# Value pages of the sample attention in two places per chunk step instead of three: a hybrid decoder step on one core

## What is computed

```
def step(S, xs):
    u_c, w_c, attn_c, q_c, k_c, gl = xs
    v_new = u_c - w_c @ S
    o = q_c @ S + attn_c @ v_new
    S = S * jnp.exp(gl)[..., None, None] + jnp.einsum('bhck,bhcv->bhkv', k_c, v_new)
    return S, o
```

```
v_past = v_pool[page_table].reshape(db, past, HA, DVA)
a = p[:, :, 0] - lam * p[:, :, 1]
return jnp.einsum('bhk,bkhe->bqhe', a.astype(v.dtype), v)
```

## Time and profile before

| | |
|---|---|
| median of 3 runs | 2679.56 us (2677.13 to 2680.27) |
| profiled execution | 2676.61 us, span 2674.4 us |
| TensorE busy | 98% of the span, granted clock 0.995 |
| vector, scalar, GpSimd busy | 57%, 43%, 51% |
| DMA | 138 GB/s over the span |
| the chunk loop from its second step | about 597 to 743 us of the span |

### The profile page before, as it was taken

How to read it: one execution, slowest core, us unless ns; L and a number is a source line. 1 busy time by engine, 2 the same in 40 slices (tenths; PEclk the granted TensorE clock), 3 DMA queues, 4 the chain that set the end, 5 groups by cost and what they waited for, 6 DMA issues and landing times.

```text
span 2674.4 us, 46814 instructions
## 1 busy us (share of the span) xinstructions
PE 2623.7 (98%) x17245; PEld 2393.9 (90%) x17245; DVE 1522.6 (57%) x2918; ACT 1149.1 (43%) x1777; POOL 1351.6 (51%) x614
## 2 busy tenths in 40 slices
PE   8999999989999999999999999999999999999998
PEld 5886666667776999999999999999999999999998
DVE  4227868865467333343347885378863788635323
ACT  2227739955523433343333424344343432444333
POOL 0210015621011766667666776676766767665663
PEclk9999999989999999999999999999999999999999
DMA  5220057635693544444444444544444544444553
GB/s 184 69 94 9 17 167 223 205 99 157 174 287 102 160 136 137 138 139 142 141 142 134 134 142 137 147 135 137 138 129 140 145 138 138 134 134 134 157 152 94
DMA packets 457191, 368.99 MB, mean 138 GB/s; under 512 B 15501, under 2 KB 400114, under 8 KB 456732
## 3 DMA queue, kind: packets, MB, share of 16 engines
q1 hardware_dynamic: 444846, 347.05, 44.2%
q0 software_dynamic: 2992, 12.26, 1.5%
q10 hardware_dynamic: 9174, 7.22, 0.9%
HBM read 351.17 MB, written 17.14 MB: 138 GB/s over the span
## 4 chain that ended last, share of the span: by engine, by line
PE 90%; DVE 4%; ACT 2%; DMA 2%; issue 1%; SPq 0%; POOL 0%; DVEq 0%; ACTq 0%
PE bank L3035 21%; PE bank L3037 21%; PE bank L3036 21%; PE bank L1232 6%; PE bank L2527 3%; PE bank L1973 2%; PE bank L922 2%; PE bank L372 1%; PE bank L524 1%; PE bank L523 1%; PE bank L522 1%; PE bank L902 1%; PE bank L873 1%; PE bank L1863 1%; DVE tmp L2903 1%
## 5 line engine op out<-in xcount | busy, mean ns | idle before, releaser
L3494 POOL TENSOR_TENSOR wl<-wring,wh 128x1024 fp32r<-128x1024 f32 x466 | 1137.5, 2456 | 589.0 <-ACT wh L3251 588.7
L3035 PE MATMUL bank<-xh,wh 128*128 128x344 f32 x2688 | 862.7, 321 | 0.3 <-POOL wl L3494 0.3
L3037 PE MATMUL bank<-xh,wl 128*128 128x344 f32 x2688 | 858.8, 320 | 0.0
L3036 PE MATMUL bank<-xl,wh 128*128 128x344 f32 x2688 | 857.3, 319 | 0.0
L3251 ACT ACTIVATE wh<-wring 128x1024 fp32r<-128x1024 f32 x466 | 484.1, 1055 | 768.3 <-PE bank L3037 645.4
L3035 PEld LDWEIGHTS bank<-xh,wh 128*128 128x128 f32 x2688 | 505.9, 188 | 1.8 <-POOL wl L3494 0.6
L3037 PEld LDWEIGHTS bank<-xh,wl 128*128 128x128 f32 x2688 | 505.4, 188 | 0.0
L3036 PEld LDWEIGHTS bank<-xl,wh 128*128 128x128 f32 x2688 | 504.3, 188 | 1.2
L3572 DVE TENSOR_TENSOR bank<-bank,gates_tmp 128x344 f32<-128x344 f32 x132 | 69.2, 524 | 511.4 <-PE bank L3037 420.4
L3616 DVE SCALAR_TENSOR_TENSOR bank<-big,vec,bank 128x344 f32<-128x344 f32 (+1 forms) x696 | 354.7, 573 | 0.5
L3035 PE MATMUL bank<-hh,wh 128*128 128x344 f32 x1040 | 334.3, 321 | 3.2 <-DVE hl L3574 3.2
(11 more groups left out here) (463 smaller groups left out, 3118.1 us busy)
## 6 DMA issues: line engine op xcount, KB each, us to landing
wring<-in_ffn_w_down SPq DMA_DIRECT2D x132, 512.0 KB, 3.6
wring<-in_ffn_w_gate SPq DMA_DIRECT2D x131, 512.0 KB, 3.9
wring<-in_ffn_w_up SPq DMA_DIRECT2D x131, 512.0 KB, 3.8
wring<-in_conv_w_pw SPq DMA_DIRECT2D x72, 512.0 KB, 4.1
big<-in_cache_attn_k SPq DMA_DIRECT2D x128, 256.0 KB, 3.0
big<-in_cache_attn_v SPq DMA_DIRECT2D x128, 256.0 KB, 3.0
wring<-in_w_in SPq DMA_DIRECT2D x20, 512.0 KB, 4.0
park<-res_a SPq DMA_DIRECT2D x1, 4128.0 KB, 12.8
```

The lines of the kernel that those rows point to most:

```text
L3035: pe.matmul(bank_out, h, mh, start=(n == 0), stop=False)
L3036: pe.matmul(bank_out, h, ml, start=False, stop=False)
L3037: mm = pe.matmul(bank_out, l, mh, start=False, stop=(n == len(terms) - 1))
L3494: pool.tensor_tensor(wl[s % 6][:, :], raw_w[s % WQ] if raw is None else raw, wh[s % 6][:, :].bitcast(F32), ALU.subtract).then_inc(w_cut, 1)
```

## The change

From `k` = 2 on, the three groups of a step stand in two places. In steps 3, 4, 5, 7 and 8 the first place takes groups `3(k-1)` and `3(k-1)+1`, which belong to one sample, one behind the other into bank 5, the second adding onto the first; the last place keeps the third. In steps 2 and 6, where the step's first group ends a sample, the first place keeps one group and the last place takes two. The middle place and its use of bank 6 are gone, with the waits for it. The vector engine adds a bank once for two groups: two sums in each step instead of three, 17 in the program instead of 24.

```diff
+        def page_groups(pe, gs, n):
+            for g in gs:
+                page_group(pe, g, n, g == gs[0], g == gs[-1])
+
+        def groups_first(k):
+            return (3 * (k - 1),) if k % 4 == 2 else (3 * (k - 1), 3 * (k - 1) + 1)
+
+        def groups_second(k):
+            return (3 * (k - 1) + 1, 3 * (k - 1) + 2) if k % 4 == 2 else (3 * (k - 1) + 2,)
+
-        def page_group(pe, g, n):
+        def page_group(pe, g, n, begin=True, end=True):
...
-                mm = pe.matmul(bank[32 * q:32 * (q + 1), n, :], w, ring[:, pp % 4, u, :], start=True, stop=True)
+                mm = pe.matmul(bank[32 * q:32 * (q + 1), n, :], w, ring[:, pp % 4, u, :], start=begin, stop=end)
             mm.then_inc(vpage_used, STRIPS)
-        def group_copy(dve, g, n):
+        def group_copy(dve, g, n, of=1):
...
-            dve.wait_ge(vpage_used, 8 + STRIPS * (g + 1))
+            dve.wait_ge(vpage_used, 8 + STRIPS * (g + of))
...
-                page_group(pe, 3 * (k - 1), 5)
+                page_groups(pe, groups_first(k), 5)
...
-                    pe.wait_ge(oc_copied, k - 1)
-                else:
-                    pe.wait_ge(k_scaled, k + 1)
-                page_group(pe, 3 * (k - 1) + 1, 6)
...
-                pe.wait_ge(group_in, 3 * k - 2)
+                pe.wait_ge(group_in, groups_first(k)[-1] + 1)
                 values_new(k - 1)
                 left(k, 2)
-                page_group(pe, 3 * (k - 1) + 2, 2 * ((k - 1) % 2) + 1)
-                pe.wait_ge(group_in, 3 * k - 1)
+                page_groups(pe, groups_second(k), 2 * ((k - 1) % 2) + 1)
                 outputs(k - 1)
...
-                group_copy(dve, 3 * (k - 1), 5)
+                group_copy(dve, groups_first(k)[0], 5, len(groups_first(k)))
...
-                group_copy(dve, 3 * (k - 1) + 1, 6)
...
-                group_copy(dve, 3 * (k - 1) + 2, 2 * ((k - 1) % 2) + 1)
+                group_copy(dve, groups_second(k)[0], 2 * ((k - 1) % 2) + 1, len(groups_second(k)))
```

More of the change, by code:

```diff
@@ L1875, in group_copy @@
                     dve.wait_ge(bias_io, 64)
-                dve.tensor_copy(d, src).then_inc(group_in, 1)
+                dve.tensor_copy(d, src).then_inc(group_in, of)
             else:
                 dve.wait_ge(group_in, g)
-                dve.tensor_tensor(d, d, src, ALU.add).then_inc(group_in, 1)
+                dve.tensor_tensor(d, d, src, ALU.add).then_inc(group_in, of)
         def page_column_in(dve, b, n):
```

## The result

| | before | after |
|---|---|---|
| median of 5 runs each | 2677.13 us (2675.00 to 2680.27) | 2694.26 us (2690.05 to 2698.45) |
| profiled execution, its span | 2676.61, 2674.4 us | 2691.74, 2689.9 us |
| mean granted TensorE clock | 0.995 | 0.991 |

The ratio is 1.0059 (1.0047 to 1.0070): slower, by some 16 us. The prediction was +4.3 us on a median of three runs (2679.56; with five it is 2677.13), and its range ended at 2687.4, 7.8 us above that median. So it was wrong; only the sign was right.

A forecast was written before the change was run, and what follows sets the result against it. TensorE, busy 98% of the span, was taken as the bound. Moved groups +4.55, pages +0.35, vector copies -0.42, step 7 +0.44 and `outputs(7)` -0.60 gave +4.3 on 2679.56: 2683.9 us, range 2678.8 to 2687.4.

The forecast's parts named there:

- Nothing is won: Middle place, step 3: without its group `right_turned` starts earlier, but `right(3,1)` still waits until 627.41; no gain.
- Nothing later gives the time back: After the loop: TensorE is dense again, its next wait of 0.19 us moves along, so the loss stays.
- The moved groups: First or last place: a second group costs 0.91 us (0.84 to 1.00), +4.55 over steps 2 to 6.
- rival 1: Added groups at either place find room in TensorE's matmul rows and cost nothing; 2678.5 us, chance 0.12.
- The vector copies: One 0.67 us vector operation fewer per step; removes TensorE's 0.42 us wait in step 3, -0.42.
- The pages: First place, steps 3 and 7: eight pages requested together come late; waits of about 0.35 and 0.37 us.
- Rival 2: Pages come late at the first place's second half in steps 3 and 7; +8.5 us, 2688.1 us, chance 0.20.
- Step 7: Loop step 7: +0.91 for the group, +0.37 page wait, less 0.84 of earlier page waits; +0.44 us.
- Step 8: `outputs(7)` no longer waits for the middle group's sum, -0.60 us; page waits and doubled first place there net 0.
- The sum: Whole kernel: 4.55 + 0.35 - 0.42 + 0.44 - 0.60 = +4.3 us, giving 2683.9 us, +0.16%.

The follow-up runs named there:

- filled run: Changed kernel with four unread 512-column matmuls put into the emptied middle place in each of steps 2 to 7; 2682.43 us, ratio 1.0021.
- the run with the hole filled and narrow groups: Changed kernel with four unread matmuls in the middle place of steps 2 to 7 and each pair's second group cut to 8 columns; 2680.74 us, ratio 1.0016.
- the middle and last place: Page groups in two places per step, the first place given up and the middle kept, against the kernel before; 2699.05 us, ratio 1.0084.

## Why the prediction was wrong

**The step that failed** is "So the group sits in a hole that the two copies make. Take it away and ... Nothing is won." That is true, and incomplete: the emptied place stands in the sum at nothing because no copy ends earlier or later, and what TensorE's idle time there does to its clock was not asked. The hole of 0.73 us was as forecast (0.8), and in step 3 `right(k,1)` comes as long after the last rows of `left(k,1)` as before (627.61 to 629.67, and 625.35 to 627.41 in the earlier trace rows). But in the changed kernel the open hole was followed in steps 2, 4 and 5 by half clock, 1.5 us for each 3.4 us of it. Filling the hole took back some 10 of the 16 us. Step by step the changed kernel is longer than the filled one by 1.48, 0.06, 1.51, 3.08 and 0.00 us in steps 2 to 6, 6.1 together, and by 2.70 in step 7, where the idle stretch told of under **Open** is a part of it. Behind the loop one more stretch at half clock, absent from the kernel before and from the filled run, makes the 16 matmuls of the earlier trace rows last 6.56 us in place of 4.86 (4.87 in the filled run), behind a wait of 0.54 in place of 0.19. Of the 11.2 us between the two spans (2689.9 and 2678.7) these three parts (6.1, 2.7 and 1.7) make 10.5. Only the 6.1 stand right behind the hole in the trace. The last 1.7 need not come from it: with the middle sums dropped and every hole covered the same matmuls took 6.56 us too. Either way "Nothing later gives the time back" had left out that the later work can become slower.

What before had shown on this point I read too narrowly: the earlier trace rows has a hole of 1.03 us in step 8 with no fall of the clock behind it, and I took from it only how long a hole is. One hole without a fall does not tell what one in every step does.

**The moved groups**: 0.87 us each by step lengths (23.12 against 22.25), and 16 records last 1.92 against 1.06. Forecast 0.91 within 0.84 to 1.00: right. The Trainium skill (Perfetto Trace Analysis, "Identifying the Most-Contended Engine") would judge TensorE's room by the share of weight loading, beside the arithmetic done against the peak. In the filled run that was 18.08 of 23.11 us, and each added group still cost its 0.87; here the measurement decides against reading room from that share, and rival 1 falls.

**The vector copies**: the wait of 0.42 in step 3 and that of `outputs(7)` are gone, as forecast; dropping the sums alone gave 0.49 in step 3 and nothing in steps 2 and 4 to 6.

**The pages**: in step 3 the second half of the first place waited 0.39 us (filled run 0.34, forecast 0.35). In step 7 it waited 0.68 in the changed kernel and 1.38 in the filled run (forecast 0.37). Step 7 is a mis-sized term: +1.83 us in the filled run against +0.44, most of it this wait. Rival 2 had the right place and a fraction of its price. Step 8 gained 0.51 there (forecast 0.60).

**The sum**: the loop of the filled run is longer than before by 0.86 + 0.89 + 0.87 + 0.87 + 0.86 + 1.83 - 0.51 = 5.67 us. So the prediction's arithmetic holds to 1.4 us for the kernel that keeps its hole covered, most of that in step 7, and misses the other two thirds of the loss.

**Open.** In step 7 of the changed kernel TensorE stood still for 2.18 us inside `left(7,1)`, and the hole behind it, at the middle place, is not seen. What held TensorE there the profile doesn't name, and no run was made for it; with the hole of step 7 open in the run filled in steps 2 to 4 no such wait came. Why a hole brings the clock down in some steps and not in others is not settled either.

## What to carry to other kernels

Work that stands in a wait can do more than use it: here four page matmuls that cost nothing also kept TensorE's clock up, and taking them out of the wait cost twice, at their new place (0.87 us) and in the clock (1.5 us for each fall, where one came). Before a filler is moved, ask what TensorE's activity at that place is without it, and price a repeated hole by the granted clock of a run that has it, since the waits listed will show only the hole. And where a ring feeds the work, moving one consumer by a place moves the request of the next one too.

## What the runs showed of the hardware

- A hole of 0.73 us in a step in which TensorE is otherwise dense was followed about 2 to 3 us later by half clock (hole ended at 602.80, 650.83 and 675.46; half clock from about 605.7, 653.4 and 677.3). The stretches lasted 3.4 us, once 6.8. The holes ending at 628.85 and 700.79 had none behind them. In the kernel before with the hole opened, 0.55 us long, three of those in steps 2 to 6 had a stretch behind them and two had none. The Trainium skill (TensorE: Matmul & The Clock Gate, "A second HAM failure mode: psum-queue depth-cycling") tells of a kernel in which frequent short idle times between groups of matmuls made the clock swing between its two levels. The traces here show such a swing with one short hole per step of 22 us.
- 24 matmuls without use, four in each of six holes, kept the clock at 1.00 through the loop, and the time was some 10 us shorter than without them.
- Half clock also stood behind two waits for pages in the run with the hole filled and narrow groups (2.67 us, ended at 622.35, half clock from 622.9; 1.63 us, ended at 713.52, half clock from 715.1); a page wait of 1.38 us in the filled run had none behind it. With the middle and last place three of seven page waits had one (2.77, 2.67 and 3.40 us), and four had none (2.84, 2.59, 2.36 and 2.67 us). So the length of one wait doesn't decide it.
